# A split weight chunk's low part, issued one step behind its high part

## The reference

```python
def first_block(x, c, positions, ...):
    u = modulate(rmsnorm(h, g_norm_ffn1[l]), sh1, sc1)
    h = h + 0.5 * gt1 * swiglu(u, w_ffn1_in[l], w_ffn1_out[l])
    u = modulate(rmsnorm(h, g_norm_mix[l]), sh2, sc2)
    h = h + gt2 * token_mixing(u, cos, sin, ...)
    u = modulate(rmsnorm(h, g_norm_ffn2[l]), sh3, sc3)
    h = h + 0.5 * gt3 * swiglu(u, w_ffn2_in[l], w_ffn2_out[l])
    return rmsnorm(h, g_final)
```

## Time and profile before

| what | value |
|---|---|
| median of 3 runs | 2620.17 us (2618.76 to 2622.85) |
| profiled execution, its own time | 2622.8 us |
| its span | 2621.0 us |
| mean clock granted to PE, share of full | 0.973 |
| PE busy | 2491.6 us, 95% |
| DVE busy | 1863.1 us, 71% |
| ACT busy | 1104.2 us, 42% |
| DMA | 453.68 MB, mean 173 GB/s |

### The profile page before, as it was taken

The page is one execution under the profiler, slowest core; times in us unless marked ns, Lnnn a source line. Parts: engine busy times, 40 slices in busy tenths (PEclk is TensorE's granted clock), DMA queues, the critical chain, the costliest instruction groups (busy, mean ns, idle before and its releaser), DMA issues.

```text
span 2621.0 us, 39392 instructions
## 1 busy us (share of the span) xinstructions
PE 2491.6 (95%) x15574; PEld 2253.0 (86%) x15574; DVE 1863.1 (71%) x3600; ACT 1104.2 (42%) x1650; POOL 0.2 (0%) x4
## 2 busy tenths in 40 slices
PE   4998999989999999999999999999999999998998
PEld 3998989889989888787888898888998888877998
DVE  6987977778879545677887569897785444576656
ACT  3444565444453323734223572222552222645443
POOL 0000000000000000000000000000000000000000
PEclk8998999989989999999999999999999999898999
DMA  8986756758858432454443166676374332222663
GB/s 305 310 265 196 257 193 200 253 179 262 294 182 260 138 97 65 157 181 133 145 147 124 63 188 206 193 233 193 97 269 133 113 105 94 72 66 76 189 187 104
DMA packets 161383, 453.68 MB, mean 173 GB/s; under 512 B 17712, under 2 KB 21296, under 8 KB 161200
## 3 DMA queue, kind: packets, MB, share of 16 engines
q1 hardware_dynamic: 161200, 451.16, 53.4%
HBM read 450.04 MB, written 1.05 MB: 172 GB/s over the span
## 4 chain that ended last, share of the span: by engine, by line
PE 61%; DVE 4%; ACT 3%; issue 1%; DMA 0%; ACTq 0%; SPq 0%; DVEq 0%
PE PS L1116 19%; PE PS L1117 19%; PE PS L1118 19%; PE PS L1258 1%; ACT own L1323 1%; DVE own L1586 1%; PE PS L1141 1%; PE PS L1143 1%; PE PS L1304 0%; DVE X L1682 0%; DVE X L1568 0%; PE PS L1287 0%; ACT NT L1382 0%; DVE Ul L1686 0%; ACT Uh L1378 0%
## 5 line engine op out<-in xcount | busy, mean ns | idle before, releaser
L1586 DVE TENSOR_TENSOR own<-raw,own 128x1024 fp32r<-128x1024 f32 x425 | 518.3, 1221 | 315.2 <-ACT own L1323 312.9
L1116 PE MATMUL PS<-Uh,own 128*128 128x256 f32 (+1 forms) x2064 | 658.1, 319 | 44.4 <-DVE Ul L1671 22.5
L1117 PE MATMUL PS<-Ul,own 128*128 128x256 f32 (+1 forms) x2064 | 645.2, 313 | 0.0
L1118 PE MATMUL PS<-Uh,own 128*128 128x256 f32 (+1 forms) x2064 | 644.9, 312 | 0.0
L1323 ACT ACTIVATE own<-raw 128x1024 fp32r<-128x1024 f32 x425 | 443.1, 1053 | 343.4 <-PE PS L1118 311.0
L1116 PEld LDWEIGHTS PS<-Uh,own 128*128 128x128 f32 x2064 | 399.3, 193 | 77.5 <-issue 37.2
L1117 PEld LDWEIGHTS PS<-Ul,own 128*128 128x128 f32 x2064 | 400.9, 194 | 20.0 <-issue 0.2
L1118 PEld LDWEIGHTS PS<-Uh,own 128*128 128x128 f32 x2064 | 400.6, 194 | 20.2
L1116 PE MATMUL PS<-Hh,own 128*128 128x256 f32 (+1 forms) x1096 | 351.1, 320 | 5.0 <-DVE Hl L1818 3.6
L1117 PE MATMUL PS<-Hl,own 128*128 128x256 f32 (+1 forms) x1096 | 345.9, 316 | 0.0
L1118 PE MATMUL PS<-Hh,own 128*128 128x256 f32 (+1 forms) x1096 | 345.8, 316 | 0.0
(11 more groups left out here) (221 smaller groups left out, 3887.0 us busy)
## 6 DMA issues: line engine op xcount, KB each, us to landing
MODS<-in_mm SPq DMA_DIRECT2D x168, 256.0 KB, 3.6
SCR<-in_mm SPq DMA_DIRECT2D x136, 256.0 KB, 3.6
raw<-in_f0i SPq DMA_DIRECT2D x64, 512.0 KB, 3.7
raw<-in_f1i SPq DMA_DIRECT2D x56, 512.0 KB, 3.6
raw<-in_f2i SPq DMA_DIRECT2D x56, 512.0 KB, 3.5
SCR<-in_ma SPq DMA_DIRECT2D x88, 256.0 KB, 5.4
raw<-in_w1i SPq DMA_DIRECT2D x44, 512.0 KB, 4.6
raw<-in_w2i SPq DMA_DIRECT2D x44, 512.0 KB, 4.3
```

Of the source, the lines that this page charges most:

```text
L1116: e.matmul(o, ll, rh, start=start, stop=False)
L1117: e.matmul(o, lh, rl, start=False, stop=False)
L1118: return e.matmul(o, lh, rh, start=False, stop=stop)
L1586: e.tensor_tensor(low, raw[:, w.n % RING, :], high.bitcast(F32), ALU.subtract).then_inc(s["wlo"].tell(w.n), 1)
```

## The change

The item "split" is taken apart. "high" (ACT) stays where "split" was. "low" (DVE) and the "fetch" that stood behind it are put later, by a new function `low_parts()`, which empties a list of chunks whose high part has been put. It is called behind the next tile's item (in `project()`, in `wide()` and in `out_tile()`, where it acts behind the first output tile of a chunk, since the list is then empty), at the start of the next `chunk()`, again in `chunk()` if the chunk now to be used is still in the list, and at the start of `tallied()`. Nothing else changes its place in the list; no instruction is added, removed or changed.

```diff
+        self.highs = []
...
-        self.put("split", n=n)
-        self.fetch()
+        self.put("high", n=n)
+        self.highs.append(n)
         return True
+
+    def low_parts(self):
+
+        while self.highs:
+            self.put("low", n=self.highs.pop(0))
+            self.fetch()
...
     def chunk(self, name, i, lead=LEAD):
         n = len(self.stream)
         self.stream.append((name, i))
+        self.low_parts()
         while self.split <= min(n + lead, self.total - 1) and self.split_next():
             pass
         assert self.split > n
         for _ in range(2 if self.deep else 0):
             self.split_next()
+        if n in self.highs:
+            self.low_parts()
         self.background()
...
     def tallied(self, r, eps, fills):
         self.norming = True
+        self.low_parts()
...
         w = self.put(what, st=st, n=n, r=r, bank=self.bank(), **fields)
         self.used[n] = (w.id, 0)
+        self.low_parts()
         return w
...
                 self.square(self.tallies[q], mm, 0 if r is LAT and st in ("f0", "go", "f1", "f2") else FOLDED)
+        self.low_parts()
         return w
...
             w = self.put(what, st=st, n=c, k=part, f=blk, fs=tuple(tts), banks=banks, final=part == KT // per - 1)
+            self.low_parts()
...
-                if w.what == "split":
+                if w.what == "high":
...
-                elif w.what == "split":
+                elif w.what == "low":
                     on.wait_ge(s["whi"], w.n)
```

## The result

| | before | with the change |
|---|---|---|
| median | 2621.34 us (4 runs) | 2583.63 us (4 runs, 2581.63 to 2584.84) |
| ratio | | 0.9855, 95% interval 0.9842 to 0.9867 |
| span of the profiled execution | 2621.0 us | 2579.7 us |

The account below looks back on a forecast made before the run. PE was taken as the bound, busy 2491.6 of 2621.0 us. Gains of -16.3 and losses of +2.2 made -14.1 us, so 2606.1 us for the median; forecast 2599 to 2613, range 2596 to 2620.

Parts of the forecast that it names:

- the ping-pong with ACT: End of w1 and wo: DVE and ACT wait for each other; w1's round would go from 4.44 to 3.29 us.
- w1's end: End of w1 into the norm: shorter DVE rounds and sums mostly at full clock, -4.6 us (bounds -3.45 and -7).
- wo: Wo into the norm: accumulations no longer fall behind, next gate tile near 549.1 instead of 551.91, -2.8 us (bounds -1, -5).
- the signs that I had named: Next profile if right: w1 rounds near 3.3 us, gate near 247, L1671 waits 5 to 7 less, DVE idle far below 312.9.
- One sign of being wrong: ACT idle before high parts, ended by DMA, since fetches are issued up to a tile later; no size given.
- in the steady stretches I cost the change at 0: Where PE is busy back to back, a chunk's lead of three tiles hides the moved low parts: 0 us.
- Term 3: Branch stage: chunk 123's tile about 2.1 us late, but the stage's end gains; net -0.7 us (bounds -2.5 and +4).
- What gets worse: Late low parts: v tiles +0.3, gv tiles +0.9, one place each in f1 and f2 +0.5; +2.2 us in all.
- the clock: Half-clock time spared: 1.7 us behind the attention's transposes (full stretch 3.1), 1.15 us at the sums behind w1.
- The waits only change their names: Rival: PE still waits for the norm's own chain; about 2615 to 2618 us, chance 0.20.
- Low parts become late: Rival: where DVE is full, low parts come late for their tiles and the clock falls; 2629 us, chance 0.12.
- Clocks stay up too: Rival: shorter gaps also spare half clock at 393 and after w1 and wo, another 6 to 8 us; 2598, chance 0.10.

Follow-up runs that it names:

- The two kernels with products: Against the kernel before, low parts go behind their own step's modulation products: 2593.6 us; same, but those split between a norm's steps stay at high parts: 2605.6 us.
- the idle matmuls: The changed kernel with idle matmuls filling five of PE's long gaps ahead of a stage's first tile: 2584.0 us.

## Why the prediction was right or wrong

**Right: what the change is about.** DVE standing before a low part with accumulations behind it, the ping-pong with ACT, its round of 3.29 us (3.26 measured), w1's end (-5.8 against -4.6), wo (-2.5 against -2.8), the heads (-1.0). The fetches were costed at 0 and measured at 0.5 us, with an interval that reaches to 3.7. The steady stretches were costed at 0 and show no step. Of the signs that I had named, rounds of 3.3 us without a wait, the gate at 246 and DVE's idle time came as said. L1671's waits of PE did not: they should have been 5 to 7 us less and are 1.1 less, since the time at w1's end was won ahead of the sums and not ahead of the gate. One sign of being wrong appeared and cost nothing that the runs show: ACT's waits for raw chunks from DMA before high parts went from 49 to 100 us in all, as the fetches are issued later.

**Wrong: the step "in the steady stretches I cost the change at 0", as I applied it.** I looked for gains at the places where the waits of PE named an accumulation. I left out the two context LayerNorm transitions (-4.4 and -3.0 measured) and the mix (-4.3), since what ended PE's waits there were Ul, SCR and ACT. But these are written by instructions which stood in the same queues behind low parts: the releaser of a wait names the last link, not the one that was late. DVE in the kernel before, ahead of the Ul that ended PE's gap of 2.68 us at 1494.59, shows it:

```profile
1492.97 1.23 DVE L1586 TENSOR_TENSOR own<-raw,own 128x1024 fp32r<-128x1024 f32 x1 [1.43 <-ACT own L1323]
1494.12 0.42 DVE L1686 TENSOR_TENSOR Ul<-NT,Uh 128x256 fp32r<-128x256 f32 x1
```

The two kernels with products confirm it: their LayerNorm transitions differ by 5.0 us, and only the low parts between a norm's steps differ in them. These places make 11.7 of the 27 us that were missing. At the norms only part of it is the gap itself, which shrank by 1.1 and 0.5 us; most of the rest goes with the half-clock stretches of 6.8 us that had followed.

**Wrong: Term 3, the branch stage, -0.7 against -7.6.** I kept DVE's arrival at the branches as it was and moved one low part behind them. But the whole stage is DVE's, and it had held three waits of half a microsecond before low parts; DVE came to each branch earlier, the tiles of chunks 123 and 128 were late by nothing and by 0.4 us and not by 2.1 and 2.0, and the stage's end, which sets wo's start, won 3.0 us of gap and was rid of a half-clock stretch of 6.8 us. Undoing the move there costs 4 to 5 us.

**Wrong: "What gets worse", +2.2.** The v and gv tiles won 1.2 and 1.5 where I had +0.3 and +0.9, for the same reason: a bound that takes the next low part's start from the trace of before holds DVE's delays fixed, which the change removes. An output tile of f1 won 0.9 where I had +0.5. Nothing in the runs tests these places one by one.

**Partly wrong: the clock.** I counted 1.7 us for one stretch and 1.15 for the sums. The stretches at half clock behind six short gaps in the middle of stages went from 37.4 to 6.8 us in all (6.8, 6.8, 6.8, 3.4, 6.8 and 6.8 behind the scores, the transposes, the branches, the mix and the two context LayerNorms; 3.4 is left at each of the first two). The prices found above run from 1.0 to 1.7 us for 3.4, so 30.6 us less is an estimated 9 to 15 us, and PE's busy time allows 14.5. The price I had used, 3.1 for 6.8, was near: 2.5 is measured at that very place. What I missed is that each of these gaps had such a stretch behind it. Part of this is luck of the execution: the changed kernel's trace has no stretch at either norm, and three other kernels with the same gaps have one of 3.4 us at one or both.

**The rivals.** "The waits only change their names" did not happen on PE. The rule of the Trainium skill that I set beside it (Perfetto Trace Analysis, Identifying the Most-Contended Engine) is to optimise the engine with the highest occupancy first; I had read it as giving nothing for a change that touches only an engine which is busy for 71%, and the measurement says 1.45%. "Low parts become late" happened: PE still waits for them six times, the longest 2.1 us, but no more than before. "Clocks stay up too" was the nearest, with 2598 still 14 us too high. The other rule of the Trainium skill that was weighed, that PE stays warm while DVE evacuates (TensorE: Matmul & The Clock Gate, Loop structure matters more than you think), has a wait of 8 us as its example; here the clock fell behind gaps of 2.35 us at the transposes and of 1.54 us at a norm, and behind the same gaps in other kernels it did not.

The profile of the idle matmuls adds a limit: a tile took nearly as long at either clock where the norm fed it.

## What to carry to other kernels

On an engine that takes its instructions in order, an instruction that waits for another engine should stand behind everything that is ready and that someone else waits for; standing behind a single ready operation of 0.7 us was worth 15 us here, and behind the last output tile it did better than behind the first. When such a wait is taken away, cost every short gap of the bottleneck engine in the neighbourhood, whatever its named releaser, and allow for the clock that may fall behind it. Idle time before the moved instruction (here 244 us less, for 41 us) is no measure of the gain, since it can turn up again at the engine's next wait.

## What the runs showed of the hardware

At the two context LayerNorms the granted clock fell to half behind all gaps of PE from 1.90 to 2.68 us (12 places), behind 5 of 8 gaps of 1.53 or 1.54 us and behind 1 of 6 of 0.77 us; the same gap was followed by half clock in one kernel and not in another, and what decides between them stays open. In stretches that PE bounds, 6.8 us at half clock cost 2.4 and 2.5 us, and 3.4 us cost 1.0 to 1.7. Behind a long gap the same half clock cost nearly nothing (2584.0 against 2583.6 us with 34 us less of it), since the tile was fed at the pace of the norm. Idle matmuls on data that is ready, into a bank that is overwritten anyway, held the clock at full behind one of five gaps and shortened the half clock behind the other four. How much of the gain the clock gave is an estimate, 9 to 15 of 41 us in the trace; the medians of the kernels that tested it could not resolve 2 us.
